# Moving two column sums of the modulation weights out of the convolution norm's chain on VectorE

## The chip, the core and the metric

One core of a Trainium2 chip runs the whole program once. The metric is the device time of one execution in microseconds (us), smaller is better. TensorE (PE) does the matrix products, VectorE (DVE) and ScalarE (ACT) the elementwise work, GpSimd (POOL) and SyncE (SP) mostly issue transfers from the chip's memory (HBM).

## The reference

The kernel is one decoder block for 256 tokens of width 2048, in float32. What matters here is its first half:

```
mod = silu(c) @ w_ada + b_ada                 # 6 vectors of 2048: shift, scale, gate, twice
h = rms_norm(x) * (1 + sc_m) + sh_m
proj = h @ w_in
y_attn = diff_attention(proj[..., :3072], ...)
y = depthwise_conv(glu(proj[..., 3072:])) + conv_b
y_conv = silu(layer_norm(y, ln_g, ln_b))      # over 1024 channels
mix = concat(y_attn, y_conv) @ w_out
x = x + gt_m * rms_norm(mix, g_post_mix)
h = rms_norm(x) * (1 + sc_f) + sh_f           # then the PEER experts, which take the rest of the time
```

The shift `sh_f` and the scale `sc_f` are needed only after `mix` is done, the gate `gt_m` while `mix` is finished.

## The kernel before

**Two streams of weights.** `w_ada` comes in blocks of 1 MB (128 x 2048 float32) into a ring of four slots (`mod_slots`, shown as `raw`). From the 33rd block on, GpSimd issues these loads: it waits until a slot is free (`mod_used`) and issues the next (L465). The blocks of the output product, `w_front`, are as large and have a ring of four slots of their own (`w_slots`, shown as `early`); SyncE issues a load each time that TensorE is done with a block (`w_used`, L360). So each use of a block releases the load of the block four places on in the same ring.

**A column sum.** For `sh_f` and `sc_f` the block lies with one output column per partition. One VectorE instruction multiplies it by `silu(c)` and adds up along the row, in place (L1427, 128 x 2048), and a short one reads the sum; the sum's end frees the slot. There are 32 such sums, numbered 0 to 31. Sums 0 to 3 stand among the gate's steps, the sums from 4 on in the stretch of this change and behind it. A call `column_sums(a, b)` makes sums a to b - 1.

**The convolution norm's chain.** VectorE sums the eight channel chunks of the squares (L1527), TensorE adds over the partitions (L1102), VectorE makes the variance (L1581), ScalarE takes the root (L621), VectorE its reciprocal (L1585) and scales the chunks in two halves (L1589), and ScalarE applies gain, bias and SiLU, chunk by chunk (L624). Each chunk counts up `z_ready`.

**The output product on TensorE.** `mix_step(half, j)` multiplies by block j of one half of the output columns: 16 matrix instructions of 128 x 512 (L1121). For the first half, steps 0 to 2 use attention heads, steps 3 to 6 use the convolution's chunks and wait for `z_ready`, step 7 uses the last heads. Between steps 6 and 7 stand eight instructions (L1150) that add up the mixing gate over the partitions. VectorE multiplies that sum by a gain (L1599, four products, `gate_made`), and does so **behind sum 18**, since its instructions run in the order in which they are written. TensorE waits for `gate_made` before `mix_step(1, 0)`, because the second half writes to the same banks of PSUM. The eight steps of the second half follow, then the norm of the result on VectorE and ScalarE (`gate_tile`, L1607), and the query product.

All orders are written out by hand in each engine's program; nothing is scheduled by a planner.

Of the kernel before, what the change touches and what calls it, by code (L numbers as in the profile page):

```python
# [119 lines left out]
def build_block(nc, x, c, c_row, w_ada, w_gate_f, b_cols, g_cols, rows, w_front, lambdas, g_subln, conv_w,  # L120
                conv_vecs, peer_wq, peer_keys, peer_u, u_rows, peer_v, out):
    with ExitStack() as ctx:
# [1225 lines left out]
        def _(dve):  # L1348
# [8 lines left out]
            def bcast_t(v, n=KC):  # L1357
                return v[:, None, :].to_broadcast([P, n, T])
# [64 lines left out]
            def column_sum(nth):  # L1423

                n, group, k = MOD_AT[nth], (nth // A_FFN) * 2 + nth % 2, (nth % A_FFN) // 2
                dve.wait_ge(*mod_arrived(n))
                dve.tensor_tensor_reduce(mod_slots[n % SLOTS], mod_slots[n % SLOTS], c_all, 1.0, 0.0, ALU.mult, ALU.add,  # L1427
                                         macc[:, group, k:k + 1]).then_inc(mod_used, 1)
# [13 lines left out]
            def column_sums(a, b):  # L1442
                for nth in range(a, b):
                    column_sum(A_FFN + nth)
# [71 lines left out]
            def heads_variance(p):  # L1516

                dve.wait_ge(o_ss, 2 * p + 2)
                dve.tensor_scalar(o_st[:, :], o_st[:, :], 1.0 / P, EPS, ALU.mult, ALU.add).then_inc(o_var, 1)
# [6 lines left out]
            def sum_channels(src):  # L1526
                dve.tensor_reduce(stat[:, 1, :], src.rearrange("p c t -> p t c"), AXX, ALU.add).then_inc(chan_sum, 1)  # L1527
# [19 lines left out]
            for p in range(1, PAIRS):  # L1547
# [28 lines left out]
            head_combine(HEADS - 1)  # L1576
            dve.wait_ge(ln_sq, 1)
            sum_channels(conv_sq)
            column_sums(5, 7)
            dve.wait_ge(ln_sum, 2)  # L1580
            dve.tensor_scalar(stat[:, 1, :], ps[:, 3, 0:T], 1.0 / (P * CONV_CHUNKS), EPS, ALU.mult, ALU.add)\  # L1581
                .then_inc(ln_var, 1)
            column_sums(7, 8)
            dve.wait_ge(ln_root, 1)
            link(dve.reciprocal(stat[:, 1, :], stat[:, 1, :]))  # L1585
            dve.wait_ge(ln_cent, 1)
            for half in range(2):
                chans = convT[:, 4 * half:4 * half + 4, :]
                dve.tensor_tensor(chans, chans, bcast_t(stat[:, 1, :], 4), ALU.mult).then_inc(ln_n, 1)  # L1589
            column_sums(8, 11)  # L1590
            heads_variance(PAIRS - 1)
            column_sums(11, 12)
            heads_scale(PAIRS - 1)
# [402 lines left out]
```

## Time and profile before

| | |
|---|---|
| median of 3 runs | 1833.39 us (1832.21 to 1834.75) |
| the profiled execution's own time | 1831.69 us |
| its span, first to last instruction | 1829.7 us |
| PE busy | 1792.3 us (98%) |
| DVE busy | 1586.5 us (87%) |
| ACT busy | 824.2 us (45%) |
| mean granted TensorE clock | 0.998 of full speed |

The busy time of an engine is the time in which one of its instructions was running; the span is what all engines share. The stretch of this change lies from 342 to 394 us of the span.

### The profile page before, as it was taken

To read this page: it belongs to the slowest core of one execution; us is meant where nothing else is said; L and a number is where in the kernel's file an instruction comes from. 1 tells how busy PE (TensorE), PEld (TensorE's weight loads), DVE (VectorE), ACT (ScalarE), POOL (GpSimd) and SP (SyncE) were. 2 spreads that over 40 slices of the span, in tenths; PEclk is the share of its full clock that TensorE was granted. 3 is DMA by queue.
4 is the path that set the end of the run, shared out by engine and by line. 5 is a ranking of instruction groups with operands and counts; after the bars stand their busy time and mean duration, and the time that the engine had idled before them with its cause. 6 is when DMAs were issued, how large, how long until landed. Compare 5 with 4: busy or idle time off the path is not lost.

```text
span 1829.7 us, 29108 instructions
## 1 busy us (share of the span) xinstructions
PE 1792.3 (98%) x9962; PEld 1571.9 (86%) x9962; DVE 1586.5 (87%) x2605; ACT 824.2 (45%) x1187; POOL 207.4 (11%) x193
## 2 busy tenths in 40 slices
PE   6999999999999999999999999999999999999998
PEld 6878888445999999999999999997888888888886
DVE  4668899966778999999999999998888888888887
ACT  3011222302635554333566666664555555555544
POOL 1000000110000000110122111121111111111110
PEclk9999999999999999999999999999999999999999
DMA  9998766798686667988899999999999999999994
GB/s 385 420 422 339 278 253 252 283 422 356 253 323 247 239 240 251 376 330 329 333 347 371 362 357 363 364 359 378 385 366 370 365 369 372 366 370 365 371 372 206
DMA packets 98193, 617.98 MB, mean 338 GB/s; under 512 B 13233, under 2 KB 21969, under 8 KB 26449
## 3 DMA queue, kind: packets, MB, share of 16 engines
q1 hardware_dynamic: 61456, 415.26, 59.0%
q0 software_dynamic: 25408, 184.58, 26.5%
q10 hardware_dynamic: 11266, 17.32, 2.5%
q8 instruction: 38, 0.62, 0.1%
q14 instruction: 25, 0.20, 0.0%
HBM read 600.26 MB, written 16.79 MB: 337 GB/s over the span
## 4 chain that ended last, share of the span: by engine, by line
PE 77%; DVE 10%; DMA 9%; issue 3%; ACT 1%; SPq 0%; DVEq 0%; ACTq 0%
PE ps L1320 30%; PE ps L960 15%; PE ps L967 9%; DMA raw<-in_w_ada 6%; PE ps L1005 6%; PE ps L1121 5%; PE ps L1175 4%; PE ps L1272 2%; PE ps L1016 2%; DVE big L1402 2%; DVE raw L1427 1%; DVE w_low L1380 1%; DMA big<-in_w_gate_f 1%; DVE big L1483 1%; DMA raw<-in_peer_v 1%
## 5 line engine op out<-in xcount | busy, mean ns | idle before, releaser
L673 ACT ACTIVATE w_hi<-raw 128x1024 fp32r<-128x1024 f32 x520 | 551.0, 1060 | 492.6 <-PE ps L1320 239.4
L1380 DVE TENSOR_TENSOR w_low<-raw,w_hi 128x1024 fp32r<-128x1024 f32 x520 | 632.9, 1223 | 89.6 <-ACT w_hi L673 82.8
L1320 PE MATMUL ps<-w_hi,a 128*128 128x512 f32 x1536 | 390.2, 389 | 0.5 <-issue 0.3
L960 PE MATMUL ps<-a,w_hi 128*128 128x384 f32 x1856 | 374.2, 343 | 0.9 <-issue 0.8
L1320 PEld LDWEIGHTS ps<-w_hi,a 128*128 128x128 f32 x1536 | 288.3, 188 | 60.9 <-ACT w_hi L673 0.5
L960 PEld LDWEIGHTS ps<-a,w_hi 128*128 128x128 f32 x1856 | 316.0, 189 | 1.9 <-issue 1.7
L1320 PE MATMUL ps<-w_low,a 128*128 128x512 f32 x1024 | 274.3, 390 | 1.2 <-DVE w_low L1380 1.2
L967 PEld LDWEIGHTS ps<-a,w_low 128*128 128x128 f32 x1856 | 238.1, 191 | 7.7 <-DVE w_low L1380 7.4
L967 PE MATMUL ps<-a,w_low 128*128 128x192 f32 x1856 | 241.3, 272 | 2.9 <-DVE w_low L1380 2.5
L1320 PEld LDWEIGHTS ps<-w_low,a 128*128 128x128 f32 x1024 | 191.9, 188 | 42.2 <-DVE w_low L1380 2.6
L1427 DVE CUSTOM_DVE_ANT_0 raw<-raw,big 128x2048 f32<-128x2048 f32 x64 | 146.2, 2290 | 67.0 <-DMA raw<-in_w_ada 64.3
L472 POOL DMA_INDIRECT big<-in_u_rows,row_ix x64 | 85.2, 1331 | 699.9 <-DVE dots_now L1402 401.4
L1402 DVE CUSTOM_DVE_ANT_0 big<-big 128x1024 f32<-128x1024 f32 x128 | 156.3, 1221 | 2.1 <-DMA big<-in_u_rows,row_ix 1.5
L989 PE MATMUL ps<-big,early 128*128 128x256 f32 x512 | 113.6, 381 | 5.9 <-ACT big L522 5.9
L989 PEld LDWEIGHTS ps<-big,early 128*128 128x128 f32 x512 | 96.3, 190 | 22.9 <-issue 10.5
L1121 PE MATMUL ps<-early,big 128*128 128x512 f32 x256 | 112.7, 600 | 2.4 <-ACT big L624 2.4
L1005 PE MATMUL ps<-big,early 128*128 128x256 f32 x512 | 113.0, 380 | 0.0
L1005 PEld LDWEIGHTS ps<-big,early 128*128 128x128 f32 x512 | 96.4, 190 | 13.5 <-issue 1.0
L1121 PEld LDWEIGHTS ps<-early,big 128*128 128x128 f32 x256 | 49.0, 192 | 62.9 <-issue 62.8
L1483 DVE SCALAR_TENSOR_TENSOR big<-big 128x256 f32<-128x256 f32 x240 | 96.5, 481 | 0.0
L1861 DVE SCALAR_TENSOR_TENSOR big<-early,row_act,big 128x1024 f32<-128x1024 f32 x64 | 81.9, 1279 | 0.0
L1861 DVE SCALAR_TENSOR_TENSOR big<-big,row_act 128x1024 f32<-128x1024 f32 x62 | 79.3, 1279 | 0.0
(227 smaller groups left out, 1683.6 us busy)
## 6 DMA issues: line engine op xcount, KB each, us to landing
raw<-in_peer_u SPq DMA_DIRECT2D x128, 1024.0 KB, 6.0
raw<-in_peer_v SPq DMA_DIRECT2D x128, 1024.0 KB, 7.0
early<-in_w_front SPq DMA_DIRECT2D x56, 1024.0 KB, 9.1
raw<-in_w_ada POOLq DMA_DIRECT2D x48, 1024.0 KB, 8.2
raw<-in_w_ada SPq DMA_DIRECT2D x32, 1024.0 KB, 12.6
raw<-in_peer_wq SPq DMA_DIRECT2D x16, 1024.0 KB, 4.8
big<-in_w_gate_f SPq DMA_DIRECT2D x16, 1024.0 KB, 7.0
gel_saved<-stage ACTq DMA_DIRECT2D x64, 192.0 KB, 7.0
```

Source lines behind the costliest of these rows:

```text
L673: act.activation(w_hi[:, h % 2, :], raw[:, s % RING, :], ACT.Copy).then_inc(hi_ready, 1)
L960: done = pe.matmul(ps[:, b % 2, 0:2 * TD].rearrange("p (m t) -> p m t", m=2), w_hi[:, ph.nth(j) % 2, k * P:(k + 1) * P], a_pair[:, kc, :, ...
L967: done = pe.matmul(ps[:, b % 2, 0:TD], w_low[:, s % RING, k * P:(k + 1) * P], a_hi[:, kc, 0:TD], start=False, stop=False, skip_group_check ...
L989: done = pe.matmul(ps[:, b // 2, (b % 2) * T:(b % 2 + 1) * T], w_slots[n % SLOTS][:, b * P:(b + 1) * P], hT[:, k, :], start=k == 0 and b % ...
L1005: done = pe.matmul(ps[:, e % 2, 0:T], w_slots[n % SLOTS][:, kc * P:(kc + 1) * P], hT[:, kc, :], start=kc == 0, stop=kc == KC - 1)
L1121: done = pe.matmul(ps[:, (MIX_FIRST, MIX_SECOND)[half][bank], :], mixed(place)[:, tt * P:(tt + 1) * P], w_slots[n % SLOTS][:, cols:cols + ...
L1320: done = pe.matmul(ps[:, 4 * tt + 2 * (j % 2) + n, :], a, w[:, n * 512:(n + 1) * 512], start=i is None and blk == 0 and m in (0, 2), stop= ...
L1380: dve.tensor_tensor(w_low[:, s % RING, :], raw[:, s % RING, :], w_hi[:, h % 2, :].bitcast(F32), ALU.subtract).then_inc(lo_ready, 1)
L1402: d = dve.tensor_tensor_reduce(got[buf][:, cols], got[buf][:, cols], h_tok[:, cols], 1.0, 0.0, ALU.mult, ALU.add, dots_now[:, n, half:half ...
L1427: dve.tensor_tensor_reduce(mod_slots[n % SLOTS], mod_slots[n % SLOTS], c_all, 1.0, 0.0, ALU.mult, ALU.add, macc[:, group, k:k + 1]).then_i ...
L1483: dve.scalar_tensor_tensor(convT[:, ch, :], upad[:, ch, j:j + T], conv_wt[:, ch, j:j + 1], convT[:, ch, :], ALU.mult, ALU.add).then_inc(ta ...
L1861: d = dve.scalar_tensor_tensor(acc[:, cols], got[n][:, cols], row_act[:, bass.ds(at(i, 4, n), 1)], acc[:, cols], ALU.mult, ALU.add)
```

## The change

VectorE's program makes the same instructions in another order. Sums 6 and 7, of which one stood ahead of the variance and one behind it, now stand behind the scaling of the chunks.

```diff
             sum_channels(conv_sq)
-            column_sums(5, 7)
+            column_sums(5, 6)
             dve.wait_ge(ln_sum, 2)
             dve.tensor_scalar(stat[:, 1, :], ps[:, 3, 0:T], 1.0 / (P * CONV_CHUNKS), EPS, ALU.mult, ALU.add)\
                 .then_inc(ln_var, 1)
-            column_sums(7, 8)
             dve.wait_ge(ln_root, 1)
             link(dve.reciprocal(stat[:, 1, :], stat[:, 1, :]))
             dve.wait_ge(ln_cent, 1)
             for half in range(2):
                 chans = convT[:, 4 * half:4 * half + 4, :]
                 dve.tensor_tensor(chans, chans, bcast_t(stat[:, 1, :], 4), ALU.mult).then_inc(ln_n, 1)
-            column_sums(8, 11)
+            column_sums(6, 11)
```

On VectorE, the order before, from the end of sum 5 on (a sum is the pair of L1427: `raw` is the slot, `macc` the result):

```order
L1427 ISA raw,macc<-raw,big 128x2048
L1427 ISA macc 128x1
L1581 TENSOR_SCALAR big<-ps 128x256
L1427 ISA raw,macc<-raw,big 128x2048
L1427 ISA macc 128x1
L1585 RECIPROCAL big<-big 128x256
L1589 TENSOR_TENSOR big<-big 128x1024 x2
```

The same place in the changed kernel, where the lines behind the removed one are numbered lower by one:

```order
L1581 TENSOR_SCALAR big<-ps 128x256
L1584 RECIPROCAL big<-big 128x256
L1588 TENSOR_TENSOR big<-big 128x1024 x2
L1427 ISA raw,macc<-raw,big 128x2048
L1427 ISA macc 128x1
L1427 ISA raw,macc<-raw,big 128x2048
L1427 ISA macc 128x1
```

Both sums went behind the two scaling instructions. On TensorE, ScalarE, GpSimd and SyncE the order is as it was. GpSimd's loads number 10 and 11, which wait for the ends of sums 6 and 7, keep their place in its program.

## Rows read from the trace of the kernel before

**Rows 1.** TensorE's waits from 341 to 455 us: in total, times, longest

```profile
PE ps L1121 <- ACT big L624: 2.4, 1, 2.4
```

**Rows 2.** Timeline of PE: start us, us, engine, line, operation, count, [idle before <- releaser]

```profile
349.95 0.39 PE L1058 MATMUL ps<-big 128*128 128x128 f32 x2
352.72 15.67 PE L1121 MATMUL ps<-early,big 128*128 128x512 f32 x32 [2.38 <-ACT big L624]
368.22 0.60 PE L1065 MATMUL ps<-ident,big 128*128 128x128 f32 x4
...
382.39 3.60 PE L1150 MATMUL ps<-early,ones 128*128 128x512 f32 x8
385.83 61.96 PE L1121 MATMUL ps<-early,big 128*128 128x512 f32 x144
```

**Rows 3.** Timeline of DVE around the chain and around the gate's products

```profile
344.17 2.29 DVE L1427 CUSTOM_DVE_ANT_0 raw<-raw,big 128x2048 f32<-128x2048 f32 x1
346.39 0.08 DVE L1427 DVE_READ_ACCUMULATOR2_ANT macc<- 128x1 f32 x1
346.39 0.42 DVE L1581 TENSOR_SCALAR big<-ps 128x256 f32<-128x256 f32 x1
...
348.93 1.75 DVE L1585 RECIPROCAL big<-big 128x256 f32<-128x256 f32 x1
350.71 2.36 DVE L1589 TENSOR_TENSOR big<-big 128x1024 f32<-128x1024 f32 x2
352.99 2.28 DVE L1427 CUSTOM_DVE_ANT_0 raw<-raw,big 128x2048 f32<-128x2048 f32 x1
...
384.94 2.29 DVE L1427 CUSTOM_DVE_ANT_0 raw<-raw,big 128x2048 f32<-128x2048 f32 x1 [2.35 <-DMA raw<-in_w_ada]
387.16 0.08 DVE L1427 DVE_READ_ACCUMULATOR2_ANT macc<- 128x1 f32 x1
387.16 2.48 DVE L1599 TENSOR_TENSOR big<-ps,big 128x512 f32<-128x512 f32 x4
```

**Rows 4.** Timeline of ACT: root, table load for SiLU, first SiLU

```profile
346.84 0.42 ACT L621 ACTIVATE big<-big 128x256 f32<-128x256 f32 x1 [4.64 <-DVE big L1581]
347.27 1.28 ACT L624 ACT_TABLE_LOAD   x1
351.97 4.04 ACT L624 ACTIVATE big<-big 128x256 f32<-128x256 f32 x8 [3.42 <-DVE big L1589]
```

**Rows 5.** Stretches: busy us (count) of PE, PEld, DVE, ACT, POOL, then PEclk, DMA share, GB/s

```profile
354.00:356.00 2.00, 2.00 (x4) 0.76 (x3) 2.00 (x3) 2.00 (x6) 0.42 (x1) 0.50 0.99 418
356.00:358.00 2.00, 2.00 (x5) 0.84 (x4) 2.00 (x3) 1.80 (x6) 0.32 (x2) 0.66 0.69 193
...
364.00:384.00 20.00, 20.00 (x51) 9.07 (x50) 11.71 (x12) 0.69 (x1) 3.16 (x6) 1.00 1.01 423
```

**Rows 6.** Timeline of POOL: loads number 9 and 10 of `w_ada`

```profile
344.55 0.53 POOL L465 DMA_DIRECT2D raw<-in_w_ada  x1 [10.02 <-DVE macc L1427]
346.76 0.53 POOL L465 DMA_DIRECT2D raw<-in_w_ada  x1 [1.68 <-DVE macc L1427]
```

**Rows 7.** SyncE's queue: two loads of `w_front`, one answer each

```profile
349.70 0.33 SPq L360 DMA_DIRECT2D early<-in_w_front  x1
...
382.59 0.33 SPq L360 DMA_DIRECT2D early<-in_w_front  x1
```

**Rows 8.** DMA queues (q0 `w_ada`, q1 `w_front`) from 379 to 384 us: packets, MB, share

```profile
q0 software_dynamic: 145, 1.06, 50.8%
q1 hardware_dynamic: 134, 1.05, 50.3%
```

**Rows 9.** Timeline of DVE at the end of the output product: sum 30, first gated tile

```profile
433.04 2.29 DVE L1427 CUSTOM_DVE_ANT_0 raw<-raw,big 128x2048 f32<-128x2048 f32 x1 [0.19 <-DMA raw<-in_w_ada]
...
437.53 1.47 DVE L1607 TENSOR_TENSOR big<-ps,big 128x512 f32<-128x512 f32 x2 [2.18 <-PE ps L1121]
```

**Rows 10.** TensorE's waits from 455 us to the end, the longest group

```profile
PE ps L967 <- DVE w_low L1380: 2.5, 7, 0.7
```

## The prediction

> **What bounds the kernel now.** TensorE is busy for 98% of the span, so I first list its waits in the stretch of the change. There is one of any size: 2.4 us, in which the output product waits for ScalarE's SiLU [rows 1]. The timeline of TensorE gives it a place: the values of the last head begin at 349.95 and take 0.39, so TensorE is free at 350.34, and step 3 of the output product begins 2.38 later at 352.72 [rows 2]. Behind 455 us the largest group of waits holds 2.5 us in seven pieces [rows 10]. So whatever TensorE gains or loses up to 455 us comes out at the end nearly whole.
>
> The wait is dearer than its 2.38 us. Behind it the granted clock is 0.50 from 354 to 356 us and 0.66 from 356 to 358 [rows 5], which is TensorE's 1.2 GHz level for most of the stretch; it was idle just before. Steps 3 and 4 take 368.22 - 352.72 = 15.50 us [rows 2]. The nine steps behind the gate's sums take 61.96 / 9 = 6.88 each at 2.4 GHz, so two take 13.76. The lost clock cost 1.74 us.
>
> Then I ask what sets the chain that ends in this wait (VectorE's timeline), and what else the moved instructions release (the transfers, the stretches with DMA share). VectorE is never idle in the chain: sum 6 runs before the variance, sum 7 between variance and reciprocal [rows 3]. But from 364 to 384 us the DMA share is 1.01 at 423 GB/s [rows 5], and VectorE waits for blocks of `w_ada`: 2.35 us before sum 18 at 384.94 [rows 3]. In that stretch the sums run at the pace of the transfers.
>
> **What the change takes away.** A sum costs 346.39 - 344.17 = 2.22 us from start to start [rows 3]. The variance then starts at 344.17 instead of 346.39. The root followed its start by 0.45 and takes 0.42 [rows 4], so it is done at 345.04; before, this lay under sum 7, now VectorE waits for it. With a tenth for the signal the reciprocal starts at 345.1 instead of 348.93, 3.8 earlier. The scaling follows 350.71 - 348.93 = 1.78 later, at 346.9, and the first SiLU 1.26 behind that, at 348.1 instead of 351.97 [rows 3, 4]. Its table load of 1.28 comes right after the root and ends at 346.4, still hidden. TensorE started 0.75 behind the first SiLU's start, so the chunk is ready at 348.9 and TensorE, free at 350.34, has 1.4 us to spare. The wait of 2.38 goes, and with it the 1.74 of the clock. Each later chunk needs a SiLU of 4.04 / 8 = 0.5 us and half a step of TensorE lasts 3.4, so no second wait follows there. From here to the gate's sums TensorE runs 4.12 us ahead: it is done with step 7 at 385.83 + 6.88 - 4.12 = 388.59 instead of 392.71.
>
> **What the change adds.** The scaling takes 352.99 - 350.71 = 2.28, so sums 6 and 7 start at 349.2 and 351.4, sum 8 at 353.6 instead of 352.99. VectorE itself is only 0.6 later. The loads are another matter: GpSimd issued load 10 at 346.76, 0.37 behind the end of sum 6 [rows 6]. Sum 6 now ends at 351.4, so load 10 is issued at 351.8, 5.0 later, and load 11 as much behind sum 7, about 4.6 later. Behind them GpSimd has its whole line of loads for sums 12 to 31, and VectorE waits for those.
>
> Is a later issue a later landing? A 1 MB block takes 1.049 / 0.421 = 2.5 us of all the bandwidth. Before, load 9 was issued at 344.55 and moved until about 349, and load 10, load 11 and the block of `w_front` issued at 349.70 [rows 6, 7] kept the engines full until some 356.5; from 356 to 358 they moved 193 GB/s, so about 1.1 us of bandwidth was free [rows 5]. Now after load 9 nothing is on the way until 351.4, the block of 349.70 plus the 1.7 us that it takes until bytes flow (my estimate from load 9, whose bytes flow late in 345). That is 2.6 us of bandwidth lost, of which the free 1.1 gives back its part: **1.5 us** net, from there on with full engines.
>
> Second, TensorE now consumes `w_front` 4.1 us earlier, and SyncE's loads move up by as much: the one at 382.59 [rows 7] to 378.5. From 379 to 384 both queues have work and move 1.06 and 1.05 MB [rows 8]: a block of `w_front` takes half of the bandwidth for 5 us, 2.5 us of what `w_ada` had to itself. Moved up, that block's transfer falls ahead of load 18's landing, where before it lay behind it. I take the whole **2.5 us**. The lower bound is the mean: 4.1 / 6.88 of a block, 0.6 MB, 1.5 us. The Trainium skill, page "DMA: Bandwidth & Descriptors", section on queues, rings and completion order, says that each engine takes turns between the queues that have work. By that rule the cost is the 2.5, by the mean 1.5; the even split in the row bears the rule out.
>
> So sum 18 comes 1.5 + 2.5 = 4.0 us later, and with it the gate's products behind it: they end at 387.16 + 2.48 = 389.64 now [rows 3], then at 393.6. TensorE, which had finished step 7 three microseconds behind them and never waited, arrives at 388.6 and **waits 5 us**. It starts the second half at 393.7, before at 392.71: 1.0 later. The 4.1 us are given back and one more.
>
> And the clock. An idle of 2.38 us was followed by half the clock for a cost of 1.74 [rows 2, 5]; after 5 us I charge the same 1.74. Bounds: nothing, if the clock stays up; twice as much, 3.5, if it comes back later after the longer gap.
>
> What the second half still allows: before, VectorE was done with sum 30 at 435.3 and waited until 437.53 for TensorE [rows 9]. TensorE comes 2.7 later, and the backlog of transfers is no worse than at sum 18, so that VectorE is not late by more than its 2.2 plus the 2.7. The rest moves as one piece.
>
> Sum: -2.38 - 1.74 (first wait) + 5.1 (new wait) + 1.74 (its clock) = **+2.7 us**. Against the profiled execution's own 1831.69 that is 1834.4. This execution lay 1.7 under the median of the runs shown, 1833.39; the median should go to 1836.1.
>
> **The rivals.** A measurement of this kernel can tell about 0.2% from no change, 3.7 us.
>
> *The transfers catch up.* If only the 1.5 us of lost bandwidth reaches sum 18, the products end at 391.1 and TensorE waits 2.6. With the clock kept that is 391.2 - 392.71 = -1.5 us (1831.9), with the clock lost +0.2. If nothing reaches it, TensorE waits for 389.7 alone and gains 3.0 (1830.4). Speaking for it: bandwidth was free around 357. Against: full engines from 364 on. Chance 0.23. To be over 0.2% faster the gate's products must not hold TensorE at all, so that nearly all 4.12 stay (1829.3): 0.05 of these.
>
> *The slow side: sum 18 is later than I think.* The transfers' delay decides over the sign of a measurable change: with 1.74 of clock, from 392.71 + 2.0 on, which means products ending at 394.6, a delay of 5.0 instead of 4.0. A second block of `w_front` that falls ahead of load 18 (2.5 more) gives +5.2, 1838.6; a clock that stays down for twice the cost gives +4.4, 1837.8. For it: load 18 had no slack at all. Against: the free 1.1 us may not be all. Chance 0.30.
>
> *The chain is not shortened,* because something other than the two sums holds the SiLU. Every link of it is in rows with no idle time of VectorE, so I give 0.04; the time would be 1833.4 and a little more.
>
> *My forecast,* waits exchanged: 0.43, with a range of its own of 1834.5 to 1837.
>
> **How the numbers follow.** Faster by over 0.2%: 0.05. Slower by over 0.2%: the slow side and a little of the forecast's edge, 0.32. Same: the rest, 0.63. The low end, 1831.0, takes in the rival in which the transfers catch up with the clock kept; the high end, 1839.5, takes in a second block and part of a longer low clock.
>
> **What the profile of the changed kernel would show.** No wait of L1121 for the SiLU and the clock at full speed from 353 to 358, with the first SiLU at 348.1. The two steps 3 and 4 in 13.8 us. GpSimd's load 10 at 351.8 and hardly any bytes from 349 to 351. Sum 18 starting near 389, and a new wait of TensorE of 3 to 7 us for VectorE's gate products, with a low clock behind it. What would make this wrong: gate products ending before 389 (then a gain of 3 to 4), or a TensorE that waits but starts the second half ahead of 392 with its clock up.

## The result and the profile after

| | before | after |
|---|---|---|
| median of 8 runs each | 1833.33 us | 1837.37 us |
| ratio, 95% interval | | 1.0025 (1.0015 to 1.0035) |
| span of the profiled execution | 1829.7 us | 1834.3 us |

The changed kernel is slower by 4.0 us, 0.25%. In the profiles the difference is there at the end of the output product already: its last norm's first products on TensorE (L1167, eight of them) begin at 447.63 us before and at 452.39 after, 4.8 later, of a span that grew by 4.6.

TensorE's timeline of the changed kernel, to be read beside [rows 2]:

```profile
350.32 0.39 PE L1058 MATMUL ps<-big 128*128 128x128 f32 x2
350.55 13.90 PE L1121 MATMUL ps<-early,big 128*128 128x512 f32 x32
364.56 0.66 PE L1065 MATMUL ps<-ident,big 128*128 128x128 f32 x4
...
382.22 7.03 PE L1121 MATMUL ps<-early,big 128*128 128x512 f32 x16
394.47 58.09 PE L1121 MATMUL ps<-early,big 128*128 128x512 f32 x128 [5.22 <-DVE big L1598]
452.39 1.05 PE L1167 MATMUL ps<-big 128*128 128x128 f32 x8
```

The wait for the SiLU is gone, and the row of steps 3 and 4 lasts 13.90 us instead of 15.67 [rows 2]. TensorE is 3.6 us ahead when step 7 begins (382.22 against 385.83); the whole stretch of this profile starts 0.4 us later (the values of the last head at 350.32 against 349.95), so that the order itself is worth 4.0. Then it waits 5.22 us for the gate's products, and starts the second half at 394.47 against 392.71.

VectorE's timeline of the changed kernel, beside [rows 3, 9], first the chain, then sum 18 and the products, then sum 30 and the first gated tile:

```profile
344.54 0.42 DVE L1581 TENSOR_SCALAR big<-ps 128x256 f32<-128x256 f32 x1
345.45 1.75 DVE L1584 RECIPROCAL big<-big 128x256 f32<-128x256 f32 x1 [0.48 <-ACT big L621]
347.24 2.36 DVE L1588 TENSOR_TENSOR big<-big 128x1024 f32<-128x1024 f32 x2
349.51 2.28 DVE L1427 CUSTOM_DVE_ANT_0 raw<-raw,big 128x2048 f32<-128x2048 f32 x1
...
365.76 2.29 DVE L1427 CUSTOM_DVE_ANT_0 raw<-raw,big 128x2048 f32<-128x2048 f32 x1 [2.43 <-DMA raw<-in_w_ada]
...
389.71 2.29 DVE L1427 CUSTOM_DVE_ANT_0 raw<-raw,big 128x2048 f32<-128x2048 f32 x1 [0.81 <-DMA raw<-in_w_ada]
...
391.93 2.48 DVE L1598 TENSOR_TENSOR big<-ps,big 128x512 f32<-128x512 f32 x4
...
435.08 2.29 DVE L1427 CUSTOM_DVE_ANT_0 raw<-raw,big 128x2048 f32<-128x2048 f32 x1 [2.67 <-DMA raw<-in_w_ada]
...
442.29 1.47 DVE L1606 TENSOR_TENSOR big<-ps,big 128x512 f32<-128x512 f32 x2 [4.91 <-PE ps L1121]
```

The reciprocal now waits 0.48 us for the root, the scaling is 3.5 us earlier. From sum 12 (365.76) on nearly every sum waits for its block; before, this began with sum 14. Sum 18 begins 4.8 us later than before and the products with it.

GpSimd's loads 9 to 11 in the changed kernel, beside [rows 6]:

```profile
344.92 0.53 POOL L465 DMA_DIRECT2D raw<-in_w_ada  x1 [10.01 <-DVE macc L1427]
352.10 0.53 POOL L465 DMA_DIRECT2D raw<-in_w_ada  x1 [6.65 <-DVE macc L1427]
354.31 0.53 POOL L465 DMA_DIRECT2D raw<-in_w_ada  x1 [1.69 <-DVE macc L1427]
```

Stretches of the changed kernel (columns as in [rows 5]); the last number is the bandwidth used, the third from the right the granted clock:

```profile
348.00:350.00 2.00, 2.00 (x7) 0.88 (x6) 2.00 (x3) 1.50 (x4) 0.00 (x0) 1.00 0.65 274
350.00:352.00 2.00, 2.00 (x11) 1.28 (x10) 2.00 (x3) 2.00 (x6) 0.00 (x0) 1.00 0.47 90
...
392.00:394.00 2.00, 0.00 (x0) 0.00 (x0) 2.00 (x6) 0.00 (x0) 0.53 (x1) 0.87 1.00 418
394.00:396.00 2.00, 1.53 (x2) 0.83 (x3) 2.00 (x2) 1.18 (x4) 0.00 (x0) 0.50 1.01 414
...
398.00:400.00 2.00, 2.00 (x4) 0.93 (x3) 0.83 (x2) 0.00 (x0) 0.53 (x1) 0.50 1.02 426
400.00:402.00 2.00, 2.00 (x5) 0.84 (x5) 1.10 (x1) 0.00 (x0) 0.00 (x0) 0.92 1.01 422
```

Between 350 and 352 us the transfers ran at 90 GB/s.

The bytes that each stream had moved by 385 us, where sum 18 started before, show what it was short of. DMA queues from 344 to 385 us (columns as in [rows 8]: q0 is `w_ada`, q1 `w_front`; packets, MB, share), first the kernel before:

```profile
q0 software_dynamic: 1542, 11.30, 69.1%
q1 hardware_dynamic: 576, 4.19, 24.5%
```

The changed kernel:

```profile
q0 software_dynamic: 1344, 9.84, 60.7%
q1 hardware_dynamic: 652, 4.82, 29.2%
```

`w_ada` is 1.46 MB short, 3.5 us at 0.421 MB per us of full engines. Of these, 0.83 MB (2.0 us, of which 0.4 is the later start of this profile) were not moved at all: bandwidth lay idle. The other 0.63 MB (1.5 us) went to `w_front`. The first share stays the same if the stretch ends at 384 or 386; the second is 1.0 and 2.0 us there, since a block of `w_front` is under way.

Behind the new wait TensorE ran at the 1.2 GHz level to just past 400 us: the eight steps of the second half took 452.39 - 394.47 = 57.92 us instead of 8 x 6.88 = 55.04.

### The profile page after: what moved, and what is told of

Its sections match the earlier page's. It is cut to its first block, busy times and chain, and to the rows that moved or that the text cites. A ratio compares the mean times of both kernels' runs of the same rounds, so it can differ in the third digit from the quotient of the medians.

```text
span 1834.3 us, 29108 instructions
## 1 busy us (share of the span) xinstructions
PE 1793.1 (98%) x9962; PEld 1570.6 (86%) x9962; DVE 1586.6 (86%) x2605; ACT 824.4 (45%) x1187; POOL 209.1 (11%) x193
## 4 chain that ended last, share of the span: by engine, by line
PE 75%; DVE 11%; DMA 9%; issue 3%; ACT 1%; SPq 0%; DVEq 0%; ACTq 0%
PE ps L1320 31%; PE ps L960 15%; PE ps L967 9%; DMA raw<-in_w_ada 7%; PE ps L1005 6%; PE ps L1175 4%; PE ps L1121 3%; PE ps L1272 2%; PE ps L1016 2%; DVE raw L1427 2%; DVE big L1402 2%; DVE w_low L1380 1%; DMA big<-in_w_gate_f 1%; DVE big L1483 1%; PE ps L934 1%
## 5 line engine op out<-in xcount | busy, mean ns | idle before, releaser
L1427 DVE CUSTOM_DVE_ANT_0 raw<-raw,big 128x2048 f32<-128x2048 f32 x64 | 146.1, 2291 | 68.5 <-DMA raw<-in_w_ada 65.8
```

## The experiments

All times below are from one profile of each kernel. "Ratio" compares all timed runs with runs of the kernel before on the same chip. Executions of one program differ: those of the kernel before took from 1829.2 to 1838.9 us, and profiles drift apart behind the stretch (last section). So where the stretch of the change is at issue, the end of the output product is the sharper measure.

| kernel | sum 18 starts | wait for the products | second half starts | it ends | ratio (95%) |
|---|---|---|---|---|---|
| before | 384.94 | none | 392.71 | 447.63 | |
| before again | 387.28 | 0.65 | 392.03 | 447.07 | |
| changed | 389.71 | 5.22 | 394.47 | 452.39 | 1.0025 (1.0015 to 1.0035) |
| changed again | 389.41 | 5.35 | 394.17 | 450.90 | |
| products behind sum 16 | 389.08 | none | 388.6 | 444.15 | 0.9993 (0.9984 to 1.0002) |
| three front loads held | 384.84 | 0.94 | 389.59 | 444.63 | 0.9987 (0.9977 to 0.9998) |
| before, loads 10 and 11 late | 386.81 | none | 392.3 | 447.26 | 1.0008 (0.9998 to 1.0017) |
| before, warm wait | 383.86 | none | 391.0 | 445.95 | 0.9999 (0.9989 to 1.0008) |
| one sum moved | 388.10 | 3.88 | 392.85 | 450.60 | 1.0015 (1.0005 to 1.0024) |
| gate waited for by banks | 388.50 | 3.23 | 391.55 | 448.25 | 1.0006 (0.9995 to 1.0016) |
| products behind 16, tile early | 388.75 | none | 388.4 | 443.33 | 0.9985 (0.9976 to 0.9994) |
| all of it, with the hold | 386.02 | none | 388.7 | 443.64 | 0.9985 (0.9976 to 0.9994) |
| before, front loads held | 379.83 | none | 392.5 | 447.43 | 1.0000 (0.9990 to 1.0009) |

"It ends" is the start of the last norm's first products (L1167 before), the first thing on TensorE behind the second half. A start of the second half with one decimal is that of step 7 plus a step of 6.88, since the trace merges the steps where nothing waits.

### The gate's products earlier

Against the changed kernel:

```diff
-            column_sums(12, 19)
+            column_sums(12, 17)
             (the four products)
-            column_sums(19, 22)
+            column_sums(17, 22)
```

> The changed kernel with the gate's four products behind sum 16 instead of behind sum 18. My theory (the loads of w_ada come late, and TensorE waits only because the products stand behind sum 18): in the changed kernel sum 16 ends at 384.5 us and the sums over the partitions of the gate on TensorE near 386, so the products end near 388.5, before TensorE is done with step 7 at 389.2. No wait of L1121 for the products, no low clock; TensorE keeps what the change gained up to the second half, which starts at 389.2. Sum 30 ends no earlier than in the changed kernel (437.3), so the first gated tile waits for VectorE there and gives 1 to 2 us back. Time 2 to 4 us below before. Rival (it is the bandwidth that bounds the stretch, wherever the products stand): VectorE's late sums hold TensorE up again at the end of the second half by all of it, time as before or above.

TensorE's timeline of this kernel:

```profile
381.71 61.96 PE L1121 MATMUL ps<-early,big 128*128 128x512 f32 x144
444.15 1.13 PE L1167 MATMUL ps<-big 128*128 128x128 f32 x8 [0.47 <-DVE big L1664]
...
452.24 0.94 PE L1167 MATMUL ps<-big 128*128 128x128 f32 x6 [1.16 <-DVE big L1664]
```

All nine steps run in one piece at full clock, though sum 18 is as late as in the changed kernel (389.08). So the new wait hangs on the place of the products behind sum 18. The waits of 0.47 and 1.16 at the first tile (before: none and 0.45) are what the late sums take back, 1.2 us as expected. The output product ends 3.5 us ahead of before. The median fell by 1.1 us, the profile's span by 1.8; the interval reaches from 2.9 us below to 0.4 above, so "2 to 4 us below" held in the trace, while the time neither reached it nor rules it out.

### Three loads of `w_front` held back

Against the changed kernel:

```diff
+                    held = W_OUT + 8 <= n < W_OUT + 11
-                    sp.wait_ge(w_used, n - SLOTS + 1)
+                    sp.wait_ge(w_used, n - SLOTS + 1 + held)
```

> The changed kernel, but SyncE issues three loads of w_front (the first three blocks of the second half that it would fetch while sums 14 to 18 wait) one step of TensorE later each. Theory: w_ada gets about one block's worth of bandwidth more before sum 18, so sum 18 starts about 2.5 us earlier than the 389.7 of the changed kernel, TensorE's wait for the gate's products shrinks from 5.2 to about 2.7 us, and the time falls by 2.5 us, by up to 4 if the clock stays up. Rival (only the lost bandwidth of the late loads 10 and 11 delays sum 18): it starts where it did, within 0.5 us, and the time is that of the changed kernel.

VectorE's timeline of this kernel at sum 18:

```profile
384.84 2.29 DVE L1428 CUSTOM_DVE_ANT_0 raw<-raw,big 128x2048 f32<-128x2048 f32 x1 [1.42 <-DMA raw<-in_w_ada]
...
387.06 2.48 DVE L1599 TENSOR_TENSOR big<-ps,big 128x512 f32<-128x512 f32 x4
```

Sum 18 came 4.9 us earlier than in the changed kernel, twice the 2.5 expected; the wait fell to 0.94 with no low clock behind it. The same order of the sums, with other transfers out of the way, is faster than before: -1.9 us (interval 0.4 to 4.2). The delay is one of bandwidth.

To see whether the hold only undoes the change, I applied it to the kernel before.

> The kernel before with the same three loads of w_front held back by one step as in the changed kernel with held loads, where sum 18 came 4.6 us earlier. Theory A (the hold takes one to two blocks out of the way of w_ada, whatever the order of the sums): sum 18 starts 3 to 4.5 us earlier than 384.9 here too, and nothing waits for it, so the time stays within 0.2%. Theory B (the hold only undoes what the change did): sum 18 stays within 1 us of 384.9.

VectorE's timeline of this kernel, sum 18 and the products, which now wait for TensorE's sums:

```profile
379.83 2.29 DVE L1428 CUSTOM_DVE_ANT_0 raw<-raw,big 128x2048 f32<-128x2048 f32 x1 [0.49 <-DMA raw<-in_w_ada]
...
385.83 2.48 DVE L1600 TENSOR_TENSOR big<-ps,big 128x512 f32<-128x512 f32 x4 [3.71 <-PE ps L1151]
```

There it moves sum 18 by 5.1 us too, a little more than theory A's 3 to 4.5, and the time stays. Theory A holds: the hold shows that the front loads set the pace of the sums, but not how much of the changed kernel's delay is due to their moving up.

### Only the loads late

Against the kernel before:

```diff
+                late = n in (MOD_GATES + 6, MOD_GATES + 7)
-                gp.wait_ge(mod_used, max(A_GATE, n - SLOTS + 1))
+                gp.wait_ge(mod_used, max(A_GATE, n - SLOTS + 1 + late))
```

> The kernel before, with VectorE's order unchanged, but GpSimd waits for one more sum before it issues loads 10 and 11 (10 behind sum 7, near 349.3; 11 behind sum 8, near 355.6). The first term by itself: bandwidth lies idle from 349 to 351. Theory: sum 18 starts 1.5 to 2.5 us later than the 384.9 of before; TensorE had 3 us to spare at the gate's products, so it does not wait and the time stays within 0.5 us. Rival (a late issue is made up by the four slots): sum 18 within 0.5 us of 384.9.

GpSimd's timeline of this kernel, load 10 and then loads 11 and 12 together:

```profile
348.94 0.53 POOL L466 DMA_DIRECT2D raw<-in_w_ada  x1 [4.22 <-DVE macc L1428]
355.21 1.05 POOL L466 DMA_DIRECT2D raw<-in_w_ada  x2 [5.75 <-DVE macc L1428]
```

Sum 18 starts at 386.81, 1.9 later, as the theory has it; the output product ends where it did. The median is 1.9 us higher; the interval, from 0.4 us below to 3.1 above, takes in the 0.5 expected and much more. The profile's extra 3.1 us arise behind 740 us. One profile of before again lies as far off at sum 18 (387.28), so that the 1.9 alone would prove little. The bytes are firmer. DMA queues of this kernel from 344 to 385 us:

```profile
q0 software_dynamic: 1472, 10.76, 65.3%
q1 hardware_dynamic: 576, 4.19, 24.4%
```

`w_front` has moved what it had before, and `w_ada` is 0.54 MB short: the late loads alone leave 1.3 us of bandwidth unused.

### The wait for the SiLU kept warm

Against the kernel before (ten products, which the profile shows as 20 rows):

```diff
             values(HEADS - 1)
+            pe.wait_ge(ln_var, 1)
+            keep_going(ps[:, 3, 0:P], 10)
             mix_step(0, 3)
```

> The kernel before, with ten small products (128 columns, results unused) on TensorE in the place of its 2.4 us wait for the SiLU. Theory: the clock stays at full speed from 354 to 358, steps 3 and 4 take 13.8 instead of 15.5 us, and the time falls by about 1.7 us, since the gate's products leave 3 us to spare. Rival (the low clock comes from something else, or small products don't keep it up): steps 3 and 4 still take 15.5 us and the time is that of before or up to 0.3 above.

TensorE's timeline of this kernel, the small products and steps 3 and 4:

```profile
350.20 2.40 PE L1095 MATMUL ps<-ones,ident 128*128 128x128 f32 x20
352.74 13.97 PE L1121 MATMUL ps<-early,big 128*128 128x512 f32 x32
```

Steps 3 and 4 take 13.8 us and the output product ends 1.7 us earlier: in the trace the theory's clock term is there. The time did not fall by the 1.7 us expected: it is that of before, with an interval (0.9989 to 1.0008) that only just takes in -1.7. The kernel before, run again, does not always have the low clock (below), so that its median may hold less than 1.7 us to gain.

### One of the two sums moved

Against the kernel before:

```diff
-            column_sums(5, 7)
+            column_sums(5, 6)
             (variance)
-            column_sums(7, 8)
+            column_sums(6, 7)
             (root, reciprocal, scaling)
-            column_sums(8, 11)
+            column_sums(7, 11)
```

> Half of the change: sum 6 stands between the variance and the root's answer, only sum 7 goes behind the scaling. Load 10 is issued as early as before (near 347), load 11 about 4 us later. The chain is one sum shorter, so TensorE's wait for the SiLU shrinks from 2.4 us to about 0.2 and its clock should stay up: TensorE is 3.9 us ahead at the gate's sums. Theory (the front blocks that move up with TensorE cost w_ada its bandwidth, the idle bandwidth of the late loads comes on top): sum 18 starts 2 to 3 us later than before, near 387.5, TensorE waits 2.5 to 3.5 us for the gate's products and starts the second half 0.5 to 1 us ahead of before; with 1.7 us of low clock the end of the output product lies 1 us behind before, without it 1 us ahead. Rival (the idle bandwidth behind loads 10 and 11 is the whole delay): sum 18 within 1 us of 384.9, TensorE waits 1 us and ends 3 us ahead.

TensorE's timeline of this kernel, the start of step 3, the second half and its end:

```profile
350.53 13.97 PE L1121 MATMUL ps<-early,big 128*128 128x512 f32 x32 [0.16 <-ACT big L624]
...
392.85 57.91 PE L1121 MATMUL ps<-early,big 128*128 128x512 f32 x128 [3.88 <-DVE big L1599]
450.60 1.05 PE L1167 MATMUL ps<-big 128*128 128x128 f32 x8
```

The wait for the SiLU shrank to 0.16 us as expected. Sum 18 at 388.10 and a wait of 3.88 speak for the theory against the rival, which had 1 us; both are somewhat above the theory's own range, and the second half started 0.1 us behind before, not 0.5 to 1 ahead. It took 57.75 us, a low clock of 2.7 us, a us more than I had charged, and ended 3.0 later. DMA queues of this kernel from 344 to 385 us:

```profile
q0 software_dynamic: 1433, 10.51, 63.8%
q1 hardware_dynamic: 656, 4.85, 29.5%
```

Here only 0.13 MB (0.3 us) less than before were moved in all, but `w_front` has 0.66 MB (1.6 us) more, as in the changed kernel. So a delay of sum 18 comes without idle bandwidth too, from the front blocks that move up with TensorE. Half of the change brings 3.0 of 4.8 us in the traces and 1.8 of 4.0 in the medians, whose intervals overlap.

### The gate waited for bank by bank

Against the changed kernel:

```diff
-            def mix_step(half, j, banks=range(4)):
+            def mix_step(half, j, banks=range(4), gated=False):
...
                     for bank in banks:
+                        if gated and k == 0:
+                            pe.wait_ge(gate_made, bank + 1)
...
-            pe.wait_ge(gate_made, 4)
-            for j in range(5):
+            mix_step(1, 0, gated=True)
+            for j in range(1, 5):
```

> The changed kernel, but TensorE waits in front of the second half for one of the gate's products at a time instead of for all four. The products are 0.6 us apart, so the second half starts 1.9 us earlier, behind a wait of 3.3 us instead of 5.2. Theory: the end of the output product moves up by at least 1.9 us against the changed kernel; by 3 to 4 if the shorter gap brings back less of the low clock (6.8 us at half clock in the changed kernel, 3.4 us behind the 2.4 us wait of before). Rival (the first bank is not what TensorE needs, it stalls on the fourth): less than 0.7 us.

Stretches of this kernel around the restart of TensorE at 391.55:

```profile
390.00:392.00 2.00, 0.45 (x1) 0.30 (x2) 2.00 (x5) 0.00 (x0) 0.53 (x1) 0.97 1.00 418
392.00:394.00 2.00, 2.00 (x4) 0.76 (x3) 2.00 (x3) 0.39 (x1) 0.00 (x0) 0.50 1.01 414
394.00:396.00 2.00, 2.00 (x5) 0.86 (x4) 2.00 (x3) 0.87 (x4) 0.31 (x1) 0.67 1.00 418
396.00:398.00 2.00, 2.00 (x6) 0.85 (x5) 1.61 (x2) 0.00 (x0) 0.32 (x2) 1.00 1.02 426
```

The wait is 3.23, the second half takes 448.25 - 391.55 = 56.70, and it ends 4.1 us ahead of the changed kernel's first profile: 2 us of shorter wait, 1.2 of clock, and 0.9 that this profile was ahead when step 7 began. The edit itself is worth 1.7: TensorE starts 0.84 us behind the start of the products (390.71) instead of 2.54; the products too came 1.2 us earlier in this profile. The 1.2 of clock can't be credited to the shorter wait: the changed kernel's second profile (below) lost the same 1.7 us behind a wait of 5.35, and this kernel ends 2.7 us ahead of it. The first bank is what TensorE needs, so the rival is out. The median is 0.6 us above before, with no change inside the interval.

### Better versions

Beside the earlier products, the first gated tile goes ahead of sum 30 (against the changed kernel; the edit of the products is not repeated):

```diff
-            column_sums(22, 2 * KC - 1)
+            column_sums(22, 2 * KC - 2)
...
             residual(1)
-            column_sums(2 * KC - 1, 2 * KC)
+            column_sums(2 * KC - 2, 2 * KC - 1)
             x2_variance(0)
             x2_diagonal(0)
+            column_sums(2 * KC - 1, 2 * KC)
```

> The changed kernel with the gate's products behind sum 16 and the first gated tile of the result ahead of sum 30. With the products alone moved, TensorE was 4.1 us ahead of before until the end of the output product and gave 1.4 us back since VectorE came to the first tile 2.6 us late (sum 30 ended at 436.0). Theory: with sum 30 behind the residual that loss falls to 0.5 us or less, TensorE is 3.5 to 4.1 us ahead at 460 us and the time is 3 to 4 us below before, plus or minus what the later phases do. Rival (VectorE has no room anywhere in the stretch): the same 2.7 us ahead as with the products alone.

VectorE's timeline of this kernel at the first tile:

```profile
431.23 2.29 DVE L1427 CUSTOM_DVE_ANT_0 raw<-raw,big 128x2048 f32<-128x2048 f32 x1 [0.18 <-DMA raw<-in_w_ada]
...
433.44 1.28 DVE L1606 TENSOR_TENSOR big<-ps,big 128x512 f32<-128x512 f32 x2
```

The tile is gated at 433.44 instead of 436.04 with the products alone moved, TensorE ends the output product 4.3 us ahead of before, and the median is 3.4 us below before (0.9985, 0.9976 to 0.9994): with nothing behind the late sums, the kernel with the change is faster than the kernel before. The kernel before was not run with these two edits. Its trace gives them nothing to gain in this stretch: TensorE does not wait for the products [rows 2] (0.65 us in its second profile), and VectorE waits 2.18 us for TensorE at the tile [rows 9]. So it is argued, not shown, that the gain is that of the shorter chain.

In the next kernel the hold of the three loads comes on top, and the four products stand behind sum 17 (`column_sums(12, 18)`) instead of behind sum 16.

> The changed kernel with the three held loads of w_front, the products behind sum 17, and the first gated tile ahead of sum 30. Theory: sum 17 ends near 383.5, the products near 386, no wait of TensorE there; 4.1 us ahead of before at the end of the output product and 3.5 to 4.1 at 460 us. Time 3 to 4 us below before. Rival (the held loads only lend bandwidth, which the sums behind 22 pay back): VectorE is late at the first tile again and TensorE 2.5 to 3 us ahead.

The product ends 4.0 ahead and the ratio is the same, so a gain by the hold does not show where no one waits for sum 18.

### The profiles' own spread

> The changed kernel once more, for the spread of one profile: sum 18 within 1 us of 389.7, wait for the products 4.5 to 5.5 us, low clock of 6.8 us again, and 4.8 us behind before at 458 us within 0.5.

TensorE's timeline of this execution, the second half and its end:

```profile
394.17 56.90 PE L1121 MATMUL ps<-early,big 128*128 128x512 f32 x128 [5.35 <-DVE big L1598]
450.90 1.05 PE L1167 MATMUL ps<-big 128*128 128x128 f32 x8
```

Sum 18 and the wait came back within 0.3 us. The clock did not: the second half took 56.73 us, a loss of 1.7 instead of 2.9, and so it ended 3.3 behind before and not 4.8. One execution took 1836.19 us.

> The kernel before once more, for the same purpose: sum 18 within 1 us of 384.9, step 3 behind a wait of 2.4 us, low clock of 3.4 us.

TensorE's timeline of this execution, steps 3 and 4 and the second half:

```profile
352.93 13.97 PE L1121 MATMUL ps<-early,big 128*128 128x512 f32 x32 [2.38 <-ACT big L624]
...
392.03 55.20 PE L1121 MATMUL ps<-early,big 128*128 128x512 f32 x128 [0.65 <-DVE big L1599]
```

Here I was wrong on two of three points. The wait of 2.38 us was there, the low clock was not: steps 3 and 4 ran at full speed. TensorE began step 7 at 384.35, 1.5 us further ahead, sum 18 was 2.3 us later (387.28), and TensorE waited 0.65 for the products. So the kernel before can show this chain of effects by itself, in small. It need not: in the warm wait TensorE began step 7 as early (384.15), and sum 18 came 1.1 us earlier than before. By 385 us these two profiles had moved the same 4.33 MB of `w_front`, and `w_ada` 11.04 and 11.26 MB, 0.5 us apart, while their sums 18 start 3.4 us apart. The landing of a single block scatters by more than the bytes moved do. Even so, the five profiles with both sums moved and no hold have sum 18 between 388.5 and 389.7, and the three with the order and the loads of before between 383.9 and 387.3.

## Why the prediction was right

The time, 1837.37, lies 1.3 us over the forecast of 1836.1 and inside the range. It lies 0.4 over the 1834.5 to 1837 that I had given to my own forecast, and the change is +4.0 us where the sum had +2.7. The form was right: one wait exchanged for another. By its steps:

- *The wait for the SiLU goes.* Shown. The first SiLU starts at 348.50; the forecast had 348.1, and the whole stretch of this profile starts 0.4 later.
- *Its clock comes back, 1.74 us.* Shown in the steps (13.90 against 15.67) and with the warm wait (13.8 against 15.5 from start to start). But before again shows that the kernel before does not always pay it, so against the median of before it is worth somewhat less.
- *Load 10 is issued 5 us later and bandwidth lies idle, net 1.5 us.* Load 10 at 352.10 and the 90 GB/s from 350 to 352 are there. The bytes give 2.0 us in the first profile (0.4 of it the later start), 1.3 in the second, and 1.3 with the late loads alone (whose stretch starts 0.4 us earlier, so that it is rather 1.7). My own figures gave a little less than I wrote: from 349 to 351.4 us are 2.4 us of idle, not 2.6.
- *The front blocks that move up cost 2.5 us.* The held loads show that these blocks set the pace. With one sum moved the delay came almost without unused bandwidth. As a size 2.5 was too much, as far as the bytes tell: by 385 us `w_front` had moved 0.63 MB more in the first profile and 0.68 in the second, 1.5 and 1.6 us (1.0 to 2.0, as the stretch is cut). That is less than a whole block and lies at the mean, 1.5, which I had as the lower bound.
- *Sum 18 4.0 us later.* 4.8 in the first pair of profiles, 2.1 in the second; the means of the pairs, 389.6 and 386.1, are 3.5 apart. `w_ada` was short of 3.5 and 2.9 us of bandwidth against the first profile of before. The 4.0 is met within the scatter of single profiles, with a larger term that was probably too large; in this, its closeness is luck.
- *TensorE waits 5 us.* 5.22 and 5.35; shown to hang on the products' place by moving them.
- *The clock behind it, 1.74.* This term was sized too small: 2.9 in one profile, 1.7 in the other, 2.7 with one sum moved. I had the longer low clock as an upper bound of 3.5. It came in the first profile, where 1.0 us of it lay within the wait and cost nothing. The mean, 2.3, is 0.5 over the charge; and before paid its 1.74 in three of four profiles with that wait, 0.4 less than charged. The two could account for about 1 of the 1.3 us by which the forecast is short; that is argued from six profiles, not shown.
- *VectorE is not late at the first tile.* Shown: it waited 4.91 us there.

Of the rivals, that the transfers catch up is out, since sum 18 was late in both profiles and 1.3 us and more of bandwidth stayed unused. The slow side was half of it: the longer low clock came in one profile of two, a second front block did not (0.63 MB more, not even one of 1.05). The measured 0.25% lies just over the border of 0.2%, on the side to which I had given a chance of 0.32 against 0.63 for no change.

## What to carry to other kernels

Work that looks like filler in a chain may be what frees a buffer. Before moving it behind the chain, find the loads that its end releases, and ask who stands behind the instructions that wait for those loads; where the transfers are the bound, a gain on one engine also brings that engine's own loads forward, into the same bandwidth. Here moving the consumer that TensorE needs (the gate's products) out from behind the loads turned a loss of 4.0 us into a time that can't be told from that of before (1.1 us under it), and with a second such place cleared the time is 3.4 us under before.

## What was not expected of the hardware

**The same wait, two clocks.** Behind a wait of TensorE of 2.38 us the granted clock fell to the 1.2 GHz level in the profiles of before, before with late loads, and before with held loads (steps 3 and 4 at 15.5 us), and did not in before again (13.8). Behind waits of 5.22 and 5.35 us of one program it cost 2.9 and 1.7 us; behind 3.88 it cost 2.7, behind 3.23 1.7, behind 0.94 nothing. Added up from the granted clock, the low stretch was 6.8 us long in the changed kernel and with one sum moved, and 3.4 us in the five other profiles that had one; it cost about half of what lay outside the wait. The cost of a wait is therefore not one number for a program, and the length of the wait does not order it.

**Shifts behind the stretch.** From 740 us on, profiles drift apart with no difference in their programs there. Before with late loads was 0.5 us ahead at 743 and 3.0 behind at 1035; TensorE's waits for `w_low` (a tile that VectorE makes of each weight block there) in this stretch are 4.9 us there and 2.5 before, 2.4 of the 3.5. Two profiles of one program drift as well: before again was 0.7 us ahead of before at 742 us and 0.4 behind at 1038, changed again 1.3 ahead of changed and 0.2 behind. The line is from the waits of before with late loads from 740 to 1040 us:

```profile
PE ps L968 <- DVE w_low L1381: 4.9, 11, 0.8
```

What sets this drift was not looked into. It is why ratios of 0.1% need many runs here, and why the time of the late loads and of the warm wait could not confirm what their traces show.
